# Mixture-of-experts stage of a two-layer network: the sum over experts is read back by 32 by 32 blocks and turned by VectorE, and the second-last expert stays on the chip

## The reference, cut to the part that is touched

```python
def expert_choice_ffn(h, router, w_gate, w_up, w_down):
    cap = CAPACITY_FACTOR * t // N_EXPERTS
    aff = jax.nn.softmax(h @ router, axis=-1)
    gate, idx = lax.top_k(jnp.swapaxes(aff, 1, 2), cap)
    xs = h[bidx, idx]
    hid = silu(einsum('becd,edf->becf', xs, w_gate)) * einsum('becd,edf->becf', xs, w_up)
    y = einsum('becf,efd->becd', hid, w_down) * gate[..., None]
    return zeros_like(h).at[bidx, idx].add(y)
...
x = x + mod_l[5] * expert_choice_ffn(h_lat, ...)       # latent tokens
ctx = ctx + mod_c[5] * expert_choice_ffn(h_ctx, ...)   # context tokens, first layer only
```

## Time and profile before

| | |
|---|---|
| median of 3 runs | 2753.28 us (2751.72 to 3352.67) |
| profiled execution | 2752.78 us |
| its span, first to last instruction | 2751.0 us |
| PE busy | 2534.0 us, 92% |
| DVE busy | 1090.4 us, 40% |
| mean granted TensorE clock | 0.973 of full |

### The profile page before, as it was taken

How to read it: one execution, slowest core, us unless ns; L and a number is a source line. 1 busy time by engine, 2 the same in 40 slices (tenths; PEclk the granted TensorE clock), 3 DMA queues, 4 the chain that set the end, 5 groups by cost and what they waited for, 6 DMA issues and landing times. The chain is left out here.

```text
span 2751.0 us, 53195 instructions
## 1 busy us (share of the span) xinstructions
PE 2534.0 (92%) x23867; PEld 1812.0 (66%) x23867; DVE 1090.4 (40%) x1950; ACT 418.2 (15%) x960; POOL 245.4 (9%) x222
## 2 busy tenths in 40 slices
PE   7999989699999997999899699888879998999999
PEld 3587655497778764588636465444448767888888
DVE  4652644411111113336745423223244345434552
ACT  2122531300000002001331200000010351110000
POOL 0000001112222220001100100000010301000000
PEclk9999999799999998999999899999999999999999
DMA  7351325599999994115345699999952201222211
GB/s 312 125 178 58 119 92 229 221 361 399 399 402 402 402 403 156 48 45 164 123 137 215 252 416 416 415 417 417 417 212 92 70 15 47 91 77 92 104 71 56
DMA packets 112235, 596.17 MB, mean 217 GB/s; under 512 B 13296, under 2 KB 37296, under 8 KB 48472
## 3 DMA queue, kind: packets, MB, share of 16 engines
q1 hardware_dynamic: 96200, 559.40, 51.9%
q0 software_dynamic: 12432, 22.88, 3.3%
q10 hardware_dynamic: 3376, 10.49, 1.0%
HBM read 575.18 MB, written 16.49 MB: 215 GB/s over the span
## 5 line engine op out<-in xcount | busy, mean ns | idle before, releaser
L1238 PE MATMUL moe_ps<-room,moe_xs 128*32 128x256 f32 x9984 | 580.3, 382 | 56.7 <-DMA room<-in_experts 38.9
L1238 PEld LDWEIGHTS moe_ps<-room,moe_xs 128*32 128x32 f32 x9984 | 396.6, 110 | 237.9 <-DMA room<-in_experts 55.1
L1238 PE MATMUL moe_ps<-room,moe_hid_t 128*32 128x256 f32 x4592 | 262.6, 380 | 8.6 <-DMA room<-in_experts 6.2
L1238 PEld LDWEIGHTS moe_ps<-room,moe_hid_t 128*32 128x32 f32 x4592 | 177.9, 110 | 90.2 <-DMA room<-in_experts 16.3
L1540 DVE TENSOR_TENSOR moe_hid<-moe_silu,moe_ps 128x512 f32<-128x512 f32 x32 | 22.0, 688 | 346.5 <-PE moe_ps L1238 337.6
L1490 DVE SCALAR_TENSOR_TENSOR x_feat<-moe_ps,mod,x_feat 128x512 f32<-128x512 f32 (+1 forms) x144 | 96.0, 731 | 133.3 <-PE moe_ps L1298 104.1
L1437 ACT ACTIVATE moe_silu<-moe_ps 128x512 f32<-128x512 f32 x32 | 19.1, 597 | 767.8 <-PE moe_ps L1238 747.6
L1561 DVE TENSOR_SCALAR moe_y<-moe_ps,moe_gates 128x256 f32<-128x256 f32 x45 | 19.0, 479 | 276.2 <-PE moe_ps L1238 276.2
L1277 POOL DMA_INDIRECT acc<-moe_y,moe_rows_id x45 | 73.7, 1639 | 363.4 <-DVE moe_y L1561 354.2
L1977 PE MATMUL mlstm_psg<-h_feat,room 128*128 128x384 f32 x256 | 90.4, 497 | 1.3 <-ACT room L2073 1.3
L1749 PE MATMUL v_ps<-room,h_feat 128*128 128x256 f32 x384 | 85.9, 382 | 0.0
(11 more groups left out here) (689 smaller groups left out, 3824.1 us busy)
## 6 DMA issues: line engine op xcount, KB each, us to landing
room<-in_experts SPq DMA_DIRECT2D x365, 1024.0 KB, 27.9
moe_slot<-in_experts SPq DMA_DIRECT2D x12, 1024.0 KB
feed_f_slots<-in_ffn_gate SPq DMA_DIRECT2D x11, 1024.0 KB, 4.9
feed_f_slots<-in_ffn_up SPq DMA_DIRECT2D x11, 1024.0 KB, 4.8
feed_f_slots<-in_ffn_down SPq DMA_DIRECT2D x8, 1408.0 KB, 6.6
room<-in_ada_w SPq DMA_DIRECT2D x10, 1024.0 KB, 5.7
qk_ada_w<-in_ada_w SPq DMA_DIRECT2D x8, 1024.0 KB, 4.9
mout_ada_w<-in_ada_w SPq DMA_DIRECT2D x8, 1024.0 KB
```

The lines of the kernel that those rows point to most:

```text
L1238: mm = pe.matmul(group_ps(part, g)[32 * q:32 * q + 32], turned[:, k * GROUP:(k + 1) * GROUP], weights[:, m, q], start=(k == 0 and g != 1), ...
```

## The change

1. The DOWN weights of experts 0 to 13 of the first layer are stored with their columns in another order: quarter q now holds columns 32q to 32q + 31 of each of the 8 tiles. A 32 by 32 block of `acc0` is then what one block of x needs, turned.
2. `acc0` collects experts 0 to 13 only. After expert 13's additions have landed, ACT issues four DMAs, one for each quarter. Each goes to 32 partitions, in pieces of 1 KB, and they stand ahead of ACT's `gate(15)`.
3. DVE adds the sum to x itself: `add_sum(k)` for the 8 tiles, each a transpose in 32 by 32 blocks of 128x768 and two adds. Tiles 0 to 2 stand ahead of `hid` of expert 15, and tiles 3 to 7 behind its `hid_t`.
4. Expert 14's product is copied to SBUF by ACT, and is put on its tokens by PE as expert 15's is (`spread`). For the first batch this stands between UP 15 and DOWN 15.
5. PE's identity matmuls and `acc_tok` are gone. The banks of the end are dealt anew, and the sum of squares is in bank 5.

```diff
@@ experts_stage
-            acc_tok = K.h[:].rearrange("p k t -> p (k t)")[:, 0:nt * D].rearrange("p (t c) -> p t c", c=D)
+            blocks = K.h[:].rearrange("p k t -> p (k t)").rearrange("p (j n) -> p j n", n=QUARTER)
+            block_turns = [t.rearrange("p g c -> p (g c)") for t in (y, xs[:, 0])] if both else []
-            end_banks = [(6 + u) % 7 for u in range(len(units))] if both else (0, 1, 3, 5, 6, 4, 0, 1)
+            end_banks = (6, 7, 0, 1, 2, 3, 4, 6, 7, 0, 1, 2, 3, 4, 6, 7) if both else (0, 1, 3, 5, 6, 4, 0, 1)
+            sums_bank = 5 if both else 7
@@ gpsimd
-                    if both:
-                        add_up(LATE)
@@ tensor
-                    def sum_and_last(batch):
...
+                    def spread(e, batch, begin, end):
+                        t0, t1, s0, s1 = streams[units[batch[0]][0]]
+                        groups = range(s0 // GROUP, s1 // GROUP)
+                        for g in groups:
                             for u in batch:
                                 dt = units[u][1]
                                 quad = slice(32 * (dt // 2), 32 * (dt // 2) + 32)
+                                mm = pe.matmul(ps[:, end_banks[u], 0:span(u)],
+                                               alone_y[quad, e % 2, g, (dt % 2) * P:(dt % 2 + 1) * P],
+                                               onehot[quad, e % 2, g, 0:span(u)], start=(begin and g == groups[0]),
+                                               stop=(end and g == groups[-1]), skip_group_check=True)
+                                if end and g == groups[-1]:
                                     mm.then_inc(sig["turned"], 1)
+                    def spread_two(batch):
+                        for u in batch:
+                            bank_is_free(u)
+                        spread(LATE, batch, True, False)
+                        spread(LAST, batch, False, True)
...
                         product(pe, LAST, UP)
+                        pe.wait_ge(sig["onehot"], 2 * G)
+                        pe.wait_ge(sig["y"], LAST)
+                        pe.wait_ge(sig["silu"], EXPERTS)
+                        spread(LATE, batches[0], True, False)
                         pe.wait_ge(sig["hid_t"], EXPERTS)
-                        pe.wait_ge(sig["y"], LAST)
                         product(pe, LAST, DOWN)
-                        pe.wait_ge(sig["sum_landed"], 16)
-                        pe.wait_ge(sig["onehot"], G)
-                        sum_and_last(batches[0])
+                        pe.wait_ge(sig["last_lat"], 1)
+                        spread(LAST, batches[0], False, True)
                         pe.wait_ge(sig["last_ctx"], 1)
-                        sum_and_last(batches[1])
+                        spread_two(batches[1])
                         for b, batch in enumerate(batches):
                             token_sums(batch)
                             if b + 2 < len(batches):
-                                sum_and_last(batches[b + 2])
+                                spread_two(batches[b + 2])
@@ scalar
                     for e in range(LAST):
+                        if both and e == LATE:
+                            act.wait_ge(sig["added"], 16 * G * LATE)
+                            by_block = dram[f"acc{layer}"].rearrange("(j t q) n -> q t j n", t=GROUP, q=4)
+                            for q in range(4):
+                                act.dma_start(blocks[GROUP * q:GROUP * (q + 1)], by_block[q]).then_inc(sig["sum_landed"], 16)
                         gate(e + 1)
...
-                        act.wait_ge(sig["added"], 16 * G * LAST)
-                        act.dma_start(acc_tok, dram[f"acc{layer}"].rearrange("(t p a) c -> p t (a c)", p=P, a=4)
-                                      ).then_inc(sig["sum_landed"], 16)
+                        act.wait_ge(sig["w_used"], used_up(LATE, DOWN))
+                        act.activation(alone_y[:, LATE % 2, 0:2].rearrange("p g c -> p (g c)"), lat_ps(DOWN), ACT.Copy)
+                        act.activation(alone_y[:, LATE % 2, 2], ctx_ps(DOWN), ACT.Copy).then_inc(sig["y"], 1)
@@ vector
+                    def add_sum(k):
+                        turned = block_turns[k % 2]
+                        step(dve.transpose(turned.rearrange("p (j t) -> p j t", t=GROUP), blocks[:, :, GROUP * k:GROUP * (k + 1)]))
+                        for r, (t0, t1, _, _) in enumerate(streams):
+                            xv = K.x[:, k, t0 * P:t1 * P]
+                            step(dve.scalar_tensor_tensor(xv, turned[:, t0 * P:t1 * P], K.mod[:, layer, r, 5 * KT + k, :], xv,
+                                                          ALU.mult, ALU.add))
...
                     if both:
+                        fill_onehot(LATE)
                         fill_onehot(LAST)
                     for e in range(EXPERTS):
                         if e < LAST:
                             turn_rows(e + 1)
-                        elif not both:
+                        elif both:
+                            dve.wait_ge(sig["sum_landed"], 64)
+                            for k in range(3):
+                                add_sum(k)
...
-                        elif e < LAST:
+                        elif e < LATE:
...
                     if both:
+                        for k in range(3, KT):
+                            add_sum(k)
                         dve.wait_ge(sig["w_used"], used_up(LAST, DOWN))
@@ host
+        if layer == 0:
+            by_block = np.arange(D).reshape(KT, 4, GROUP).transpose(1, 0, 2).reshape(-1)
+            w[0:EXPERTS - 2, 2] = w[0:EXPERTS - 2, 2][:, :, by_block]
```

More of the change, by code:

```diff
@@ L1307, in bank_is_free @@
                             pe.wait_ge(sig["summed"], users[-1] + 1)
-                    def sum_and_last(batch):
-                        r = units[batch[0]][0]
-                        t0, t1, s0, s1 = streams[r]
-                        for u in batch:
-                            bank_is_free(u)
-                            for tt in range(t0, t1):
-                                pe.matmul(ps[:, end_banks[u], (tt - t0) * P:(tt - t0 + 1) * P],
-                                          acc_tok[:, tt, units[u][1] * P:(units[u][1] + 1) * P], K.ident[:], start=(tt == t0),
-                                          stop=False, skip_group_check=True)
-                        pe.wait_ge(sig["last_lat"], 1)
-                        for g in range(s0 // GROUP, s1 // GROUP):
+                    def spread(e, batch, begin, end):
+                        t0, t1, s0, s1 = streams[units[batch[0]][0]]
+                        groups = range(s0 // GROUP, s1 // GROUP)
+                        for g in groups:
                             for u in batch:
@@ L1322, in sum_and_last @@
                                 quad = slice(32 * (dt // 2), 32 * (dt // 2) + 32)
-                                mm = pe.matmul(ps[:, end_banks[u], 0:span(u)], last_y[quad, g, (dt % 2) * P:(dt % 2 + 1) * P],
-                                               onehot[quad, LAST % 2, g, 0:span(u)], start=False, stop=(g == s1 // GROUP - 1),
-                                               skip_group_check=True)
-                                if g == s1 // GROUP - 1:
-                                    mm.then_inc(sig["turned"], 1)
+                                mm = pe.matmul(ps[:, end_banks[u], 0:span(u)],
[3 more added lines that the diff above has]
+                                if end and g == groups[-1]:
+                                    mm.then_inc(sig["turned"], 1)
+                    def spread_two(batch):
[3 more added lines that the diff above has]
+                        spread(LAST, batch, False, True)
                     def last_half(half, c):
@@ L1365, in token_sums @@
                                 final = max(v for v in range(len(at_end)) if at_end[v][0] == r)
-                                mm = pe.matmul(ps[32 * q:32 * q + 32, 7, r * P:(r + 1) * P], weigh[:, dt],
+                                mm = pe.matmul(ps[32 * q:32 * q + 32, sums_bank, r * P:(r + 1) * P], weigh[:, dt],
                                                sq[:, u % 8, q * P:(q + 1) * P], start=(u == 0), stop=(u == final),
@@ L1472, in _ @@
                         rows = 32 * (t1 - t0)
-                        ins = act.activation(kept_sums[0:rows, r * P:(r + 1) * P], ps[0:rows, 7, r * P:(r + 1) * P], ACT.Copy)
+                        ins = act.activation(kept_sums[0:rows, r * P:(r + 1) * P], ps[0:rows, sums_bank, r * P:(r + 1) * P], ACT.Copy)
                     ins.then_inc(sig["sums_kept"], 1)
@@ L1534, in _ @@
                             turn_rows(e + 1)
-                        elif not both:
+                        elif both:
+                            dve.wait_ge(sig["sum_landed"], 64)
+                            for k in range(3):
+                                add_sum(k)
+                        else:
                             add_alone(LATE, batches[0])
```

## The result

| | before | after |
|---|---|---|
| median | 2751.72 us | 2772.86 us |
| profiled span | 2751.0 us | 2771.1 us |
| PE busy | 2534.0 us | 2531.3 us |

The ratio is 1.0083, 95% interval 1.0072 to 1.0093: the change costs 21 us by the medians and 23 by the ratio. One of the five runs of before took 3352.67 us and is not in the ratio. The forecast was 2766, and the range ended at 2772.

What follows compares the result with a forecast made beforehand. PE waits for weights up to 1013 us, then 5.3 us behind DOWN 15 for the sum; the late half of the DMA engines counts. Forecast: 26.3 - 13.3 = +13.0 us on 2752.78, taken as 2766; range 2759 to 2772.

Steps and rivals of the forecast that it cites:

- the end of DOWN 15: PE's last DOWN, delayed by the sum's landing, three add_sum and half clock: 1078.2 against 1051.9, +26.3 us.
- the end of the stage behind it: From DOWN 15's end to the last sum of squares: 15.4 us instead of 28.7, -13.3 us.
- the sum's own time: Time of ACT's read of the sum on a late DMA engine, 192 packets: 12.0 us, for a landing at 1056.8.
- both bounds: Limits on the sum's time: 9.6 us from 1 KB packets to 128 partitions, 14.4 from copies between 32 partitions.
- slower than both bounds: Rival: the sum's DMA read drops below 219 GB/s and lands after 1062, total 2775; chance 0.07.
- The queues: ACT's DMAs stand behind SP's issued weights or take turns with them; the total is the same either way.
- Bytes are shared evenly: Rival: four 1 KB packets go in one turn, the sum lands at 1044 to 1047, total 2753; chance 0.08.
- ACT's four issues, even if each is held up [...] cost nothing: ACT's DMA issues need be done only when hid is due at 1063.5; uncovered they would cost some 2 us.
- The small terms: Around DOWN 15: three add_sum 6.6 us, hid to PE's start 2.1, DOWN 15 10.6 + 2.0, later add_sum 1.6 to spare.

Runs made afterwards that it cites:

- no_read: The changed kernel without its four DMAs, experts 0 to 13 left out of the result; ratio 0.9956 to before, 35 us below the changed kernel.
- wide_1k: The changed kernel with one DMA of 128 partitions in 1 KB pieces for four of 32, sum added wrongly; ratio 1.0039 to before.
- own_rows: The changed kernel with the sum in its own DRAM rows, one DMA reading 24 KB for each of 128 partitions; 2744.18 us, ratio 0.9989 to before.
- adds_behind: The changed kernel with all eight add_sum behind hid_t of expert 15, none ahead of hid; ratio 1.0078 to before.
- wide_4k: The changed kernel with one DMA of 128 partitions in 4 KB pieces, sum added wrongly; ratio 0.9989 to before.
- narrow_4k: The changed kernel with four DMAs of 32 partitions in 4 KB pieces, sum added wrongly; ratio 1.0024 to before.

## Why the prediction was off in size

**Direction and way: right.** The sum's landing took the place of the wait behind DOWN 15, the end of the stage gave its part back, and the loss outweighed it. In distances to the mark, the end of DOWN 15 moved by 74.65 - 38.85 = +35.8 us (forecast +26.3), and the end of the stage behind it by 14.9 - 28.7 = -13.8 (forecast -13.3). Together +22.0 instead of +13.0.

**The step that failed: the sum's own time.** "The sum goes to 32 partitions at a time like the second and has the packets of the first [...] I take the middle, 12.0." By `no_read` the late engines end with the weights at 1009.79 + 31.9 = 1041.7 in the changed kernel, and the sum lands at 1062.15 - 0.7 = 1061.45. So its own time was **19.8 us**, outside both bounds (9.6 and 14.4). The landing is 8.6 us later behind the mark than forecast: 7.8 from this term (19.8 for 12.0), and 0.85 from the weights, which end 31.9 us behind the mark and not 31.05. That is 8.6 of the 9.5 us missed; the rest is DOWN 15 (0.6) and the three `add_sum` (0.4). The same account for `wide_1k` gives 1049.4 - 1041.2 = 8.2 us, near the lower bound. So the bound from the earlier trace rows was a fair one for 128 partitions, but the one from the earlier trace rows was no upper bound for 32 beside another queue. The Trainium skill (SBUF — State Buffer, section Door 1) gives 32 partitions half of the ports. The trace agrees in direction, but 19.8 to 8.2 is more than the factor of two.

The bounds priced the sum's packets alone. What they left out:
- A packet of the weights gets longer beside such a read: by 0.05 us in 1016 to 1032, by 0.17 in 1034 to 1040. A turn of both costs 0.327 + 0.057 - 0.281 = 0.10 us above the weights alone, and later 0.456 + 0.083 - 0.281 = 0.26, not the 0.0625 that 12.0 us for 192 packets come to.
- The last packets, on half of the engines, take 0.080 us each. That is near the 0.075 that 14.4 us for 192 come to, so the sum alone was priced nearly right by the upper bound; what goes beyond it is the price of the turns.

Of the 192 packets on a late engine about half went in turns, with some 98 of the weights: 53 at 0.10 (5.5 us), 15 at 0.26 (3.9), 14 from 1041 to 1046 at 0.1 (1.4), 14 from 1046 to 1054 at 0.2 (3.0); the other 96 alone at 0.08 (7.7). That is 21.5, some 2 us above the 19.8: an estimate, whose borders are rough and whose averages mix the two halves of the engines.

The held issue is not the reason. ACT's fourth DMA is let go only at 1046.4, and from 1042 to 1046 the two queues take 50.6% of the 16 engines (41.3 and 9.3): that is what the late half alone takes when it is never idle. So the early half had run dry, but the late half, which sets the landing, had not.

The rival "slower than both bounds" named the result ("landing after 1062 gives 2775"), for a reason that was partly this one, "the late half of the engines on few partitions". It had 0.07. Its other reason, rows 128 KB apart in DRAM, is not enough: `wide_1k` reads pieces of 1 KB that are 128 KB apart on a partition and is fast.

**The queues.** The forecast left open whether ACT's DMAs stand in line or take turns, since the landing would be the same. The turns were seen. UP 15's weights came late (1.89 us at 1039.64 was the longest of PE's waits for weights from the mark on), and it cost nothing, as UP 15 ended at 1042.4, long before the landing. The Trainium skill (DMA: Bandwidth & Descriptors, section Queues, rings and completion order) says that an engine goes round its queues packet by packet, and the traces agree: 682 to 679, and 584 to 583 with packets of 4 KB. Not every run does: `wide_1k` has 770 of the weights to 899 of the sum, and `own_rows` 276 to 142. No run explains these two. "Bytes are shared evenly" is excluded by the same rows.

**"ACT's four issues, even if each is held up [...] cost nothing": right.** The issues of the changed kernel (duration min, median, max in ns):

```profile
L1450 ACTq DMA_DIRECT2D h_feat<-acc x4: 329/558/33601, 1011.3 to 1012.8; - x4
```

The fourth was held for 33.6 us. `gate(15)` ran at 1046.5 and expert 14's matmuls at 1049.8, well ahead of 1062. The one-hot matmuls of expert 14 end at 1053.2, and DOWN 15 starts 9.05 us behind the landing; so only a landing before about 1044 would have made this a bound of its own. In `adds_behind` it is one: DOWN 15 starts as these matmuls end.

**The small terms: right.** Three `add_sum` 6.96 us (forecast 6.6; the stride of 1 KB costs the transpose nothing, 0.98); `hid` to DOWN 15 2.09 (2.1); DOWN 15 13.24 (12.6), at half clock for about 5 us. The five later `add_sum` ended at 1082.6, 1.8 us before DOWN 15 (forecast 1.6). The end of the stage took 14.9 us (15.4).

## What to carry to other kernels

A transfer that shares the DMA engines with another is priced by what *both* queues lose: take the time of the other queue's packets beside it, not the rate of the new one alone. Where queues take turns packet by packet, the size of the packets decides who gets the engines, and so a long transfer that is needed soon should be laid out in DRAM for long pieces and sent to all 128 partitions by one DMA. Here 1 KB to 4 KB gained 14 to 16 us, one DMA of 128 partitions for four of 32 gained 10 to 12, and 4 KB to 24 KB gained nothing more. When a step is put ahead of a chain's last links, all that they wait for inherits its landing, and moving the adds behind `hid_t` gave back 4 us of it at most.

## What was not expected of the hardware

- A read of 1 KB pieces to 32 partitions lengthens the packets of another queue that writes to 128 partitions, from 0.28 to 0.33 us, and to 0.46 when half of the engines do nothing but that read (1034 to 1040; 0.41 from 1046 to 1054); with 4 KB pieces to 0.41. Reads to 128 partitions leave them at 0.28. The four 32-partition DMAs were sent together, and four against one is not separated from the partitions.
- The total rate falls with it: 416 GB/s for `wide_4k` from 1016 to 1032 and 291 for `narrow_4k`.
- A run of 24 KB on both sides went in packets of 22 KB on average, 0.82 us each, and with one of them to two packets of the weights the sum's 3.12 MB moved in 12 us.
- The fourth of four DMAs with 768 packets each held its issuing engine for 33.6 us. Four of 4 KB pieces took 1.8 us together to issue, and one DMA with 3072 packets 0.4 us.
